# Dividing the softmax rows on GpSimd ahead of the transposes in a hybrid decoder layer

## The reference, cut to what matters

```python
u = rmsnorm(x) ; z = u @ w_in + b_in          # q (8 heads x 64) | k (2 x 64) | v (2 x 64) | x-branch 512 | gate branch 512
# group A: windowed attention, blocks of 128 queries against 256 keys
s = q . k / 8 - slope * dist                  # (masked outside the window)
m = max(max(s), sink) ; p = exp(s - m)
p = p / (sum(p) + exp(sink - m))              # one number per query row and head
attn = p @ v
# group B: causal conv -> RG-LRU (a scan over time) -> * gelu(gate branch)
h = x + concat(attn, lru * gelu(y)) @ w_out + b_out
y = h + (silu(gate) * up) @ w_ffn_out ; final rmsnorm
```

## Time and profile before

| | |
|---|---|
| time, median of 3 runs | 2252.71 us (2251.35 to 2252.78) |
| the profiled execution's own time | 2252.27 us |
| its span, first to last instruction | 2250.5 us |
| mean granted TensorE clock | 0.997 of full speed |
| busy: PE, DVE, ACT, POOL | 2213.5, 1156.8, 836.1, 28.3 us |
| slots and the work up to the output projection, per block | about 95 to 106 us |

### The profile page before, as it was taken

How to read it: one execution, slowest core, us unless ns; L and a number is a source line. 1 busy time by engine, 2 the same in 40 slices (tenths; PEclk the granted TensorE clock), 3 DMA queues, 4 the chain that set the end, 5 groups by cost and what they waited for, 6 DMA issues and landing times.

```text
span 2250.5 us, 29784 instructions
## 1 busy us (share of the span) xinstructions
PE 2213.5 (98%) x12213; PEld 1871.9 (83%) x12213; DVE 1156.8 (51%) x2013; ACT 836.1 (37%) x1348; POOL 28.3 (1%) x58
## 2 busy tenths in 40 slices
PE   7999999999999999999999999999999999999998
PEld 7878888888877888888877788888887899999997
DVE  5676645445366543444538554444546745444453
ACT  4674233243275322224338332223426632222223
POOL 1000000000000000000000000000000000000000
PEclk9999999999999999999999999999999999999999
DMA  7445224222534322222353422223254322222221
GB/s 265 152 163 204 83 89 151 91 94 84 207 116 167 101 95 97 94 99 82 131 181 113 169 88 97 96 85 99 87 181 151 108 100 85 85 90 82 93 84 70
DMA packets 78923, 264.81 MB, mean 118 GB/s; under 512 B 9521, under 2 KB 13825, under 8 KB 78772
## 3 DMA queue, kind: packets, MB, share of 16 engines
q1 hardware_dynamic: 73504, 246.58, 31.8%
q0 software_dynamic: 3232, 9.80, 1.3%
q10 hardware_dynamic: 2052, 6.53, 0.7%
HBM read 231.04 MB, written 32.84 MB: 117 GB/s over the span
## 4 chain that ended last, share of the span: by engine, by line
PE 92%; DVE 3%; ACT 2%; DMA 1%; issue 1%; ACTq 0%; DVEq 0%
PE bank L711 29%; PE bank L713 29%; PE bank L712 29%; PE bank L876 1%; PE bank L858 1%; PE bank L842 1%; PE bank L898 1%; DMA out_y_p<-y_tok 1%; DVE s_p L1709 1%; ACT s_p L1296 0%; PE bank L805 0%; PE bank L752 0%; DMA xs_tok<-in_x_sample 0%; PE bank L888 0%; DVE xc L1750 0%
## 5 line engine op out<-in xcount | busy, mean ns | idle before, releaser
L711 PE MATMUL bank<-x_hi,w_hi 128*128 128x512 f32 (+1 forms) x2224 | 787.1, 354 | 5.1 <-DVE x_lo L1610 3.2
L713 PE MATMUL bank<-x_hi,w_lo 128*128 128x512 f32 (+1 forms) x2224 | 779.9, 351 | 0.0
L712 PE MATMUL bank<-x_lo,w_hi 128*128 128x512 f32 (+1 forms) x2224 | 778.5, 350 | 0.0
L1181 ACT ACTIVATE w_hi<-w_raw 128x1024 fp32r<-128x1024 f32 (+1 forms) x294 | 304.6, 1036 | 994.7 <-PE bank L713 960.4
L711 PEld LDWEIGHTS bank<-x_hi,w_hi 128*128 128x128 f32 x2224 | 418.5, 188 | 72.8 <-issue 12.6
L712 PEld LDWEIGHTS bank<-x_lo,w_hi 128*128 128x128 f32 x2224 | 418.7, 188 | 57.6 <-issue 2.4
L713 PEld LDWEIGHTS bank<-x_hi,w_lo 128*128 128x128 f32 x2224 | 418.1, 188 | 56.5
L711 PE MATMUL bank<-a_hi,w_hi 128*128 128x512 f32 (+1 forms) x1168 | 412.2, 353 | 5.1 <-DVE a_lo L1797 3.8
L1569 DVE TENSOR_TENSOR w_lo<-w_raw,w_hi 128x1024 fp32r<-128x1024 f32 (+1 forms) x294 | 351.0, 1194 | 123.1 <-ACT w_hi L1181 123.1
L713 PE MATMUL bank<-a_hi,w_lo 128*128 128x512 f32 (+1 forms) x1168 | 411.6, 352 | 0.0
L712 PE MATMUL bank<-a_lo,w_hi 128*128 128x512 f32 (+1 forms) x1168 | 410.9, 352 | 0.0
(11 more groups left out here) (313 smaller groups left out, 1593.3 us busy)
## 6 DMA issues: line engine op xcount, KB each, us to landing
w_raw<-in_units SPq DMA_DIRECT2D x222, 512.0 KB, 3.2
w_raw<-in_units SPq DMA_DIRECT2D x64, 448.0 KB, 3.1
w_hi<-keep SPq DMA_DIRECT2D x51, 512.0 KB, 3.3
w_lo<-keep SPq DMA_DIRECT2D x51, 512.0 KB, 4.5
w_kept<-keep SPq DMA_DIRECT2D x30, 512.0 KB, 4.5
keep<-w_hi SPq DMA_DIRECT2D x22, 512.0 KB, 5.1
keep<-w_lo SPq DMA_DIRECT2D x22, 512.0 KB, 5.8
x_tok<-in_x_prompt POOLq DMA_DIRECT2D x12, 512.0 KB, 5.0
```

The lines of the kernel that those rows point to most:

```text
L711: nc.tensor.matmul(out, h, hi[:, kt, c0:c1], start=(first and kt == kts[0]), stop=False)
L712: nc.tensor.matmul(out, h, lo[:, kt, c0:c1], start=False, stop=False)
L713: mm = nc.tensor.matmul(out, l, hi[:, kt, c0:c1], start=False, stop=(kt == kt_of[u] - 1))
L1181: A(w_hi[:, slot(b, u), 0:n], w_raw[:, u % RAW, 0:n], ACT.Copy).then_inc(w_hi_ready, 1)
```

## The change

GpSimd gets a program for each block, `normalise`: for each attention unit it waits for the reciprocals and multiplies the four rows-by-256 tiles of `s_p` in place by them, one `tensor_scalar` a head, and reports `p_normed`. PE's transposes wait for that. `spread`, the copy to `a_tok` and the product with it are taken out; ACT and DVE read bank V directly for `a_hi` and `a_lo`, and `attend` waits for `amix_ready` where it waited for `atok_ready`. DVE takes the sums' reciprocals of unit s in slot s (before: in slot s + 1), and no longer waits for its own reciprocal. PE's transposes of unit s - 1 move from behind the branch unit of slot s to its middle (behind 4 of 8 tiles in even slots, behind the gates in odd ones; those of unit 0 stay at the end of slot 1), those of unit 7 behind one more part. ACT copies the transposes ahead of reading the branch unit. A table load for the square root that ACT did ahead of time, by a dummy `Sqrt`, is gone.

```diff
@@ GpSimd @@
+            def normalise(b):
+                for s in range(NUN):
+                    qb, jp = s // 2, s % 2
+                    rec_ready.wait(pool, b, s + 1)
+                    for hh in range(HH):
+                        head = hh // 2 * JT + 2 * jp + hh % 2
+                        ins = nc.gpsimd.tensor_scalar(s_p[:, s % 2, hh, :], s_p[:, s % 2, hh, :],
+                                                      rec[:, qb % 2, head:head + 1], None, ALU.mult)
+                    p_normed.by(ins)
             for b in range(NB - 1):
+                normalise(b)
                 amix_ready.wait(pool, b, QB)
...
             b = NB - 1
+            normalise(b)
             pool.wait_ge(smp_dve, SMP_DVE_K)
@@ TensorE, mixers @@
                 def probs_T(s):
-                    p_ready.wait(pe, b, s + 1)
+                    p_normed.wait(pe, b, s + 1)
...
-                    if s >= 2 and s % 2 == 0:
-                        recs_read.wait(pe, b, s // 2)
...
                     if jp == 0 and qb > 0:
-                        atok_ready.wait(pe, b, qb)
+                        amix_ready.wait(pe, b, qb)
-                def spread(qb):
...
                     if s >= 2:
                         attend(s - 2)
-                    if s >= 3 and s % 2 == 1:
-                        spread((s - 3) // 2)
...
-                        cut = KT - 3 if s == 1 else KT - 2
+                        cut = KT // 2 if s % 2 == 0 else KT - 3 if s == 1 else KT - 2
...
                     if s % 2 == 1:
                         gates(s // 2)
+                    if s >= 2:
+                        probs_T(s - 1)
...
-                    if s >= 1:
-                        probs_T(s - 1)
+                    if s == 1:
+                        probs_T(0)
...
                 attend(NUN - 2)
+                part(ahead[1][0], recurrent[:2], ahead[1][1])
                 probs_T(NUN - 1)
-                for m, c in ahead[1:]:
-                    part(m, recurrent[:2], c)
+                part(ahead[2][0], recurrent[:2], ahead[2][1])
                 attend(NUN - 1)
-                spread(QB - 1)
@@ ScalarE, mixers @@
-                def attn_recs(qb):
...
                 def attn_hi(qb):
-                    atok_ready.wait(act, b, qb + 1)
+                    av_done.wait(act, b, 2 * qb + 2)
                     amix_hi.by(A(a_hi[:, 0:4, qb * P:(qb + 1) * P],
-                                 a_tok[:, :].rearrange("p (c q) -> p c q", c=4), ACT.Copy))
+                                 V[:, :].rearrange("p (c q) -> p c q", c=4), ACT.Copy))
...
+                    if s >= 1:
+                        probs_T(s - 1)
                     if kind == "x":
...
-                A(std_h[:, 0:1], eps_t[:, :], ACT.Sqrt)
-                attn_recs(QB - 1)
+                attn_hi(QB - 1)
                 lru_root(LC - 1)
-                attn_hi(QB - 1)
@@ VectorE, mixers @@
                     rec_ready.by(nc.vector.reciprocal(ro, ...))
-                    rec_ready.wait(dve, b, s + 1)
-                def attn_out(qb):
...
                 def attn_lo(qb):
-                                     a_tok[:, :].rearrange("p (c q) -> p c q", c=4),
+                                     V[:, :].rearrange("p (c q) -> p c q", c=4),
...
                     if s >= 3 and s % 2 == 1:
-                        attn_out((s - 3) // 2)
                         lru_input((s - 3) // 2)
                         lru_scan((s - 3) // 2)
                         lru_mix((s - 3) // 2)
+                        attn_lo((s - 3) // 2)
...
-                    if s >= 1:
-                        softmax_2(s - 1)
...
                         conv(0)
+                    softmax_2(s)
                     if s >= 1:
                         probs_T(s - 1)
...
                 probs_T(NUN - 1)
-                softmax_2(NUN - 1)
                 lru_square(LC - 1)
-                attn_out(QB - 1)
+                attn_lo(QB - 1)
                 lru_input(LC - 1)
-                attn_lo(QB - 1)
```

More of the change, by code:

```diff
@@ L216, in hymba_layer @@
         h_prev = place("h_prev", [P, LC])
-        a_tok = place("a_tok", [P, NH * HEAD], at=[top[0]])
         ssum = place("ssum", [P, W])
@@ L374, in hymba_layer @@
         av_done = Signal(sem("av_done"), NUN)
-        atok_ready = Signal(sem("atok_ready"), QB)
         rec_ready = Signal(sem("rec_ready"), NUN)
-        recs_done = Signal(sem("recs_done"), QB)
-        recs_read = Signal(sem("recs_read"), QB)
+        p_normed = Signal(sem("p_normed"), NUN)
         amix_hi = Signal(sem("amix_hi"), QB)
@@ L602, in load_x @@
                     x_in.by(pool.dma_start(x_tok[:, m, :], x_p[0, bass.ds(b * T + m * P, P), :]))
+            p_normed.prime(pool)
+            def normalise(b):
[7 more added lines that the diff above has]
+                    p_normed.by(ins)
             nc.gpsimd.memset(eps_t[:, :], EPS).then_inc(zeroed, 1)
@@ L672, in _ @@
             for s in (gemm_done, xT_done, stath_done, alongx_done, alongh_done, staty_done, vT_done, sc_done, pT_done,
-                      av_done, recs_done,
+                      av_done,
                       gates_done, yT_done):
@@ L879, in attend @@
                     av_done.by(mm)
-                def spread(qb):
-                    rec_ready.wait(pe, b, 2 * qb + 2)
-                    for j in range(JT):
-                        for g in range(NKV):
-                            head = g * JT + j
-                            mm = nc.tensor.matmul(TB[0][g * HEAD:(g + 1) * HEAD, j * P:(j + 1) * P],
-                                                  rec[:, qb % 2, head:head + 1].to_broadcast([P, HEAD]), ident[:, :],
-                                                  start=True, stop=True, skip_group_check=True)
-                    recs_done.by(mm)
                 def gates(c):
@@ L1332, in lru_hi @@
                     lmix_hi.by(A(a_hi[:, KT - LC + c, 0:T], gl[:, c % 2, :], ACT.Copy, scale=0.5))
-                def attn_recs(qb):
-                    recs_done.wait(act, b, qb + 1)
-                    amix_ready.wait(act, b, qb)
-                    recs_read.by(A(a_tok[:, :], TB[0][:, :], ACT.Copy))
                 def attn_hi(qb):
-                    atok_ready.wait(act, b, qb + 1)
+                    av_done.wait(act, b, 2 * qb + 2)
                     amix_hi.by(A(a_hi[:, 0:4, qb * P:(qb + 1) * P],
-                                 a_tok[:, :].rearrange("p (c q) -> p c q", c=4), ACT.Copy))
+                                 V[:, :].rearrange("p (c q) -> p c q", c=4), ACT.Copy))
                 for s in range(NUN):
-                    if s >= 3 and s % 2 == 1:
-                        attn_recs((s - 3) // 2)
                     exps(s)
@@ L1545, in _ @@
                       sc_read, pTb_ready,
-                      rec_ready, atok_ready, amix_ready, xc_ready, lru_m, gelu_in, lmix_f, lmix_ready, act_f, act_ready,
+                      rec_ready, amix_ready, xc_ready, lru_m, gelu_in, lmix_f, lmix_ready, act_f, act_ready,
                       y_ready):
@@ L1730, in probs_T @@
                                                        TB[1][:, :].rearrange("p (n q) -> p n q", n=4)))
-                def attn_out(qb):
-                    recs_read.wait(dve, b, qb + 1)
-                    atok_ready.by(TT(a_tok[:, :], V[:, :], a_tok[:, :], ALU.mult))
                 def conv(c):
@@ L1823, in mixers @@
                         split(b, UH + s - 1 + RING)
-                    if s >= 3 and s % 2 == 1:
-                        attn_lo((s - 3) // 2)
                     if s == NUN - 1:
```

6 lines of the change are left out of this document (1 added, 5 removed).

## The result

The changed kernel takes 2233.72 us (median of 4 runs, 2232.71 to 2235.56) against 2252.28 us (2251.35 to 2252.78) for the kernel before on the same chip: a ratio of 0.9919, 95% interval 0.9903 to 0.9934. The forecast was 2233 us with a range of 2227 to 2244. The profiled execution took 2232.71 us with a span of 2230.9 us, which is 19.6 us less than the span of before.

The account below looks back on a forecast made before the run. PE was taken as the bound, busy 2213.5 of 2250.5 us. The terms 15.5 + 1.8 + 1.6 - 1.1 + 0.8 + 2.1 - 0.4 - 1.0 gave 19.3 us less, so 2233 us, range 2227 to 2244.

Parts of the forecast that it names:

- Spreads, 15.5 us: PE loses `spread`, 0.97 us at each of 16 places, all counted as gain: 15.5 us.
- Moved transposes, 0 us with ends of 2.4: Moving PE's transposes within the slots changes no work; new borders between matmul kinds bounded at +2.4 and -2.4 us.
- GpSimd, hidden: GpSimd's divisions, 0.5 us each (0.31 to 1.2), four a unit, hide behind PE's matmuls and cost nothing.
- unit 7's limit of 1.07 us: Unit 7, called tightest, has 4.3 us from reciprocal to transposes, so PE waits once one GpSimd instruction exceeds 1.07 us.
- the list of tight ones: Units with little cover for GpSimd: 1, 3 and 5 with about 5.3 us, 7 with 4.3; even units over 8.
- The gates: Scores of slots 4 and 6 wait for `gates_read`; shorter chain lifts slack to about 0.4 us, block 0 waits go: +1.8 us.
- First slots, +1.6 and -1.1: Blocks 1 to 3: earlier `pT` copy saves about 0.5 us each, +1.6; `softmax_2(0)` ahead of `conv_end(0)` costs 3 x 0.38, -1.1.
- Ends of the blocks: `a_lo` waits go in blocks 0 to 2, +2.1 us; block 3 -0.4, waiting about 1.8; small waits +0.8.
- The port, -1.0 us: DVE and GpSimd share a port; GpSimd's reads holding DVE up cost -1.0 us, mainly block 0, ends 0 and -6.
- GpSimd too slow: Rival: PE waits for `p_normed`; break-even at 1.6 us an instruction, about 2288 us at 2.2; chance 0.10.
- The change without effect: Rival: PE comes sooner but scores wait as much for `gates_read`, leaving only the ends: 2247 to 2252 us; chance 0.06.
- The collision: Rival: DVE and GpSimd hold each other up 0.5 to 1.0 us a unit, half the slots pass it on: 2238 to 2245; chance 0.14.

Follow-up runs that it names:

- doubled kernel: The changed kernel with a second GpSimd pass per unit, multiplying the divided rows by 1.0: 2274.93 us, ratio 1.0103 against the kernel before.
- the removal alone: The kernel before with 7 of the 8 matmuls of each spread left out and nothing moved: 2249.78 us, ratio 0.9990.

## Why the prediction was right, point by point

The mechanism is the predicted one: PE's own work was removed, and the chain behind it was shortened enough to let the gain through. That the sum came within 0.7 us (19.3 against 18.6 us from the first scores on) is partly luck, since single terms miss by up to 1.4 us and these misses cancel.

- **Spreads, 15.5 us.** Right in kind, 14.1 us in size: at the border with attend 0.09 us of each comes back. PE's busy time is 2198.6 us (foretold: near 2197), slots 3 and 5 of block 1 take 10.44 and 10.45 us (near 10.4), slot 4 takes 8.72 (near 8.7).
- **Moved transposes, 0 us with ends of 2.4.** Right: slot 4, in which of PE's work only they moved, keeps its length within 0.02 us. That their place is worth some 7 to 8 us through ACT's order was only partly foreseen: the sum had the 1.8 us of block 0 and the `pT` copies of the first slots, not that exponentials stand behind the copy.
- **GpSimd, hidden.** Right, with the size wrong: 0.92 us an instruction (median; 912 ns the least) where I took 0.5, between the ends of 0.31 and 1.2 but nearer the far one. From the reciprocal there were 5.2 to 6.0 us where I had 5.3, and 4.8 us for unit 7 where I had 4.3; it waited 0.29 us in block 0 and 0.27 us in block 3, where four instructions took 4.74 and 3.87 us. In block 1 the same 3.87 us were hidden: there unit 7 has 4.8 us, but in block 3 only 3.9 from GpSimd's start to transposes that already wait, because the parts of the output projection ahead of them are half as wide. The prediction saw this width for `a_lo`, but not for its tightest deadline. That 0.92 us still lay under unit 7's limit of 1.07 us was luck as far as the price goes. The doubled kernel shows the limit itself to be there, and placed a little too tight: for unit 3 the two passes of 7.6 us less the wait of 1.49 leave 6.1 us of cover where the prediction had 5.3. The first unit, with about 5.4 us, was not in the list of tight ones and should have been. The term for PE's waits at POOL was put at nothing and measured 0.6 us.
- **The gates.** Both shortenings are there. `softmax_1(3)` starts 637.41 - 634.73 = 2.7 us after the scores (foretold 2.6, before 3.3), ACT's `ii` ends at 644.01 + 0.69 = 644.70, 0.47 us before the next scores (foretold 0.4), and in block 0 the two waits of 0.9 us are down to about 0.15 us each, too little to stand in the list of waits: `ii` ends at 97.68 and the scores start at 97.73. So about 1.5 of the 1.8 us are gained. With GpSimd silent these two slots are 0.13 and 0.16 us shorter still. That the kernel without this shortening gains nothing is shown by the removal alone.
- **First slots, +1.6 and -1.1.** 1.1 us were gained at `attend(0)`: its wait for `pT` fell from 0.72 to 0.36 us in each of blocks 1 to 3, not by 0.5 as the sum had it. At the convolution 1.4 us were lost, of which `softmax_2(0)` is 0.38 us a block by its own length; how late the store landed moves this wait by over a microsecond (1.15 and 1.9 us in two profiles of the same kernel), which the prediction had not looked at.
- **Ends of the blocks.** The 2.1 us of blocks 0 to 2 are gained in full, and so are the 0.8 us of small waits behind slot 7 of block 0 (0.44 and 0.18 us for `pT`, 0.20 for `w_lo`). In block 3 PE comes to the last recurrent tile 1766.95 - 1758.08 = 8.9 us after the last attend began, as foretold, after a wait of 1.5 us (foretold 1.8).
- **The port, -1.0 us.** The sign is right. DVE is held up a little everywhere, about 6 us of busy time over the groups that grew, nearly all off PE's path; with GpSimd silent the kernel gains 2.0 us, the 0.6 us of waits at POOL included, so some 1.4 us is left for this term.
- **Rivals.** GpSimd too slow: not at 0.92 us, true at twice that. The change without effect: true of the removal alone. The collision: there, at 1 to 2 us, where its rival's price was 5 to 12.

## What to carry to other kernels

When work is taken off the bound engine, look at the slack of the wait that comes next on it, in the trace: here it was 0.14 us, and of the 0.66 us removed in slots 3 and 5 only 0.08 arrived (11.34 to 11.26) until the chain behind the wait was shortened too. An idle engine may take work at less than half the speed of a busy one and still win, as here with 924 against 349 ns, if its deadline is counted from the row that starts it to the row that needs it; double the work to find out how far the cover goes. Look whether a table load that stands behind a wait for a transfer can be started ahead of it. And before small gains are read from spans, take off what differs ahead of the change.

## What the runs showed of the hardware

GpSimd's `tensor_scalar` with one number per partition took 912 ns at least for 128x256 float32, 3.6 ns an element of the row, against 349 ns on DVE. The slope of its fills, 0.84 ns an element, was no guide to it. The second pass of the doubled kernel, which multiplies by a constant, took 852 ns (median). By the Trainium skill, "GPSIMD Engine Reference", § 3.1, its best loop needs 1.8 cycles an element at 1.2 GHz; the estimate from that, 256 x 1.5 = 384 ns, is far below the measured value, which decides.

DVE and GpSimd hold each other up unevenly. Timeline of DVE beside GpSimd's unit 7 of block 0, which began at 137.59:

```profile
138.01 1.22 DVE L1554 TENSOR_TENSOR w_lo<-w_raw,w_hi 128x1024 fp32r<-128x1024 f32 x1
139.14 0.69 DVE L1772 SCALAR_TENSOR_TENSOR a_lo<-gl,a_hi 128x512 fp32r<-128x512 f32 x1
```

```profile
137.59 2.94 POOL L611 TENSOR_SCALAR s_p<-s_p,rec 128x256 f32<-128x256 f32 x2 [8.57 <-DVE rec L1708]
```

Under these two-input instructions two divisions took 2.94 us instead of 1.83, and one of the 128 took 2.04 us; DVE's `w_lo` kept its 1.22 us. It is not so with every such pair. Beside the unit of 633.16 us shown above, DVE ran two instructions with two inputs as well:

```profile
633.58 1.62 DVE L1730 SCALAR_TENSOR_TENSOR xc<-xb,vec,xc 128x512 f32<-128x512 f32 x2
```

The four divisions took 3.82 us there and 3.62 without such company (unit 3), 0.2 us more. The other way round, DVE's instructions became at most 0.27 us longer: 440 against 170 ns for the four elements of `nm`, 971 against 748 ns for the convolution's end, 651 against 421 ns for the gelu's argument. The Trainium skill, "SBUF — State Buffer", § "Who interferes with whom", has the one that comes second wait for the whole of the other; the trace agrees that such pairs disturb each other, and for GpSimd behind DVE's `w_lo` and `a_lo` in the size too, but not beside the convolution's end, and a DVE instruction behind a GpSimd one of 0.92 us lost at most 0.27 us.
